# Hybrid decoder layer on one core: constant matmuls ahead of the first block, x scaled by column halves, and the last block's final weight units taken one token half after the other

## What is computed

```python
xn   = rms_norm(x, attn_norm)
proj = xn @ w_in                       # 2048 -> 7184 columns, for two groups of heads
h = x + concat(gated_deltanet(...), moba_attention(...)) @ w_o
hn = rms_norm(h, ffn_norm)
h = h + (silu(hn @ w_gate) * (hn @ w_up)) @ w_down
gate = sigmoid(rms_norm(h, ple_norm) @ w_ple_gate)
out = h + gate * (p @ w_ple_proj)      # p: 256 tokens x 256
```

## Time and profile before

| | |
|---|---|
| median of 3 runs | 1355.14 us (1354.77 to 1355.86) |
| time of the profiled execution | 1352.64 us |
| its span in the profile | 1350.9 us |
| PE busy | 1329.8 us, 98% of the span, 7295 matmuls |
| DVE busy | 797.7 us, 59% |
| ACT busy | 608.8 us, 45% |
| HBM | 237.45 MB read, 2.10 MB written, 177 GB/s over the span |

### The profile page before, as it was taken

One profiled execution on the slowest core, in us unless ns is written; L12 is line 12 of the kernel. 1 busy time (PEld: TensorE's weight loads), 2 busy tenths in 40 slices (PEclk: granted clock), 3 DMA queues, 4 the chain that ended last, 5 costly groups with the idle time before them and its releaser, 6 DMA issues.

```text
span 1350.9 us, 19215 instructions
## 1 busy us (share of the span) xinstructions
PE 1329.8 (98%) x7295; PEld 1124.1 (83%) x7295; DVE 797.7 (59%) x996; ACT 608.8 (45%) x756; POOL 60.7 (4%) x71
## 2 busy tenths in 40 slices
PE   7999999999999999999999999999999999999998
PEld 5999987887888888888888888888888888888886
DVE  6657887589667555555555554454555555555554
ACT  6456533452445545444444443434444444454442
POOL 4102000031110000000000000000000000000000
PEclk9999999999999999999999999999999999999999
DMA  7645454544444756666666656666666666555563
GB/s 240 185 148 172 144 179 134 141 140 139 128 125 141 236 184 187 192 191 180 195 192 187 185 192 193 191 198 191 195 188 189 190 187 187 181 193 188 186 198 129
DMA packets 126366, 240.52 MB, mean 178 GB/s; under 512 B 9743, under 2 KB 10050, under 8 KB 126298
## 3 DMA queue, kind: packets, MB, share of 16 engines
q1 hardware_dynamic: 125108, 237.46, 58.1%
q10 hardware_dynamic: 1190, 2.12, 0.5%
HBM read 237.45 MB, written 2.10 MB: 177 GB/s over the span
## 4 chain that ended last, share of the span: by engine, by line
PE 92%; DVE 5%; ACT 1%; issue 1%; DVEq 0%; ACTq 0%
PE pair L511 26%; PE pair L513 25%; PE pair L512 25%; PE pair L714 3%; PE pair L715 3%; PE pair L716 3%; PE bg L615 2%; DVE w_lo L1117 1%; PE bg L680 1%; PE bg L767 1%; PE bg L556 1%; ACT w_hi L835 0%; DVE mn L1351 0%; PE bg L595 0%; DVE mn L1272 0%
## 5 line engine op out<-in xcount | busy, mean ns | idle before, releaser
L1117 DVE TENSOR_TENSOR w_lo<-raw,w_hi 128x1024 fp32r<-128x1024 f32 x444 | 541.6, 1225 | 420.8 <-ACT w_hi L835 417.9
L835 ACT ACTIVATE w_hi<-raw 128x1024 fp32r<-128x1024 f32 x444 | 468.0, 1060 | 495.7 <-PE pair L513 457.5
L511 PE MATMUL pair<-w_hi,xT_hi 128*128 128x512 f32 x1088 | 431.7, 397 | 0.0
L513 PE MATMUL pair<-w_hi,xT_lo 128*128 128x512 f32 x1088 | 424.1, 390 | 0.0
L512 PE MATMUL pair<-w_lo,xT_hi 128*128 128x512 f32 x1088 | 423.7, 389 | 0.0
L513 PEld LDWEIGHTS pair<-w_hi,xT_lo 128*128 128x128 f32 x1088 | 204.2, 188 | 43.3
L511 PEld LDWEIGHTS pair<-w_hi,xT_hi 128*128 128x128 f32 x1088 | 204.4, 188 | 41.5
L512 PEld LDWEIGHTS pair<-w_lo,xT_hi 128*128 128x128 f32 x1088 | 204.5, 188 | 40.1
L511 PE MATMUL pair<-w_hi,actT_hi 128*128 128x512 f32 x352 | 137.7, 391 | 0.0
L513 PE MATMUL pair<-w_hi,actT_lo 128*128 128x512 f32 x352 | 137.1, 389 | 0.0
L512 PE MATMUL pair<-w_lo,actT_hi 128*128 128x512 f32 x352 | 137.0, 389 | 0.0
(11 more groups left out here) (223 smaller groups left out, 953.6 us busy)
## 6 DMA issues: line engine op xcount, KB each, us to landing
raw<-in_w_in_dram SPq DMA_DIRECT2D x112, 512.0 KB, 3.8
raw<-in_w_gate_dram SPq DMA_DIRECT2D x88, 512.0 KB, 4.4
raw<-in_w_up_dram SPq DMA_DIRECT2D x88, 512.0 KB, 3.8
raw<-in_w_down_dram SPq DMA_DIRECT2D x88, 512.0 KB, 4.7
raw<-in_w_o_dram SPq DMA_DIRECT2D x32, 512.0 KB, 4.9
raw<-in_w_ple_gate_dram SPq DMA_DIRECT2D x32, 512.0 KB, 4.6
raw<-in_w_ple_proj_dram SPq DMA_DIRECT2D x4, 512.0 KB, 7.4
h<-in_x_dram SPq DMA_DIRECT2D x4, 512.0 KB, 8.5
```

What stands on the lines that cost most here:

```text
L511: mm(banks[t][:], hi[:, ts], wh, start=first, stop=False)
L513: m = mm(banks[t][:], lo[:, ts], wh, start=False, stop=last)
L835: f(w_hi[j % RING][:], raw[j % RING][:], ACT.Copy).then_inc(hi_ready, 1)
L1117: v.tensor_tensor(w_lo[j % RING][:], raw[j % RING][:], w_hi[j % RING][:].bitcast(F32), ALU.subtract).then_inc(lo_ready, 1)
```

## The change

At the beginning, PE issues 5 constant matmuls (128x128 by 128x128, float32) before the transposes of `p` and 10 behind them. The units 0 to 3 are split by k tiles (two instructions of 512 columns on ACT and on DVE in place of one of 1024), and PE starts the first k tile of a block once its own low part is ready. The squares of x are made by column halves: ACT takes both of token half 1 and the first of token half 0, DVE the second of token half 0. DVE scales token half 0 and ACT token half 1, each in two column halves, and the groups x0 to x3 wait for the first halves alone, x4 to x7 for the second. POOL adds the two half sums itself. `pp` of block 2 is copied by ACT alone. The groups of transposes are spread: x0 and x1 behind the first k tile of unit 3, x2 behind its second, and x3 to x7 behind one k tile each of units 4, 5 and 6.

At the end, the last four units of the last block are taken first for token half 0 and then for token half 1, and the last token half is finished in two pieces of 256 columns, each with its own DMA.

```diff
     for g in range(KT // 2):
-        at[U_QKV - 1 + g // 4][g // 2 % 2].append(("x", g))
+        i = max(g - 1, 0)
+        at[U_QKV - 1 + i // 2][i % 2].append(("x", g))
...
+LAST_PIECES = ((0, 0, CB), (1, 0, CB // 2), (1, CB // 2, CB))
...
-            for t in range(NT):
-                sp.wait_ge(out_ready, NT * 3 + t + 1)
-                sp.dma_start(out_d[:, t, 3 * CB:], h[:, t, 3 * CB:]).then_inc(out_landed, 16)
+            for n, (t, lo, up) in enumerate(LAST_PIECES):
+                sp.wait_ge(out_ready, NT * 3 + n + 1)
+                sp.dma_start(out_d[:, t, 3 * CB + lo:3 * CB + up], h[:, t, 3 * CB + lo:3 * CB + up]).then_inc(out_landed, 16)
...
-                pool.wait_ge(x_sq[t], 1)
-                rstd(x_rs[:, t:t + 1], x_ms[:, t:t + 1], x_ss[:, t:t + 1], 1.0 / D, EPS, x_rstd, t)
+                pool.wait_ge(x_sq[t], 2)
+                g.tensor_scalar(x_ms[:, t:t + 1], x_half[t][:, 0:1], x_half[t][:, 1:2], EPS, ALU.add,
+                                ALU.add).then_inc(x_rstd, 1)
+                pool.wait_ge(x_rstd, 2 * t + 1)
+                g.tensor_tensor(x_rs[:, t:t + 1], x_ms[:, t:t + 1], half[:, 0:1], ALU.pow).then_inc(x_rstd, 1)
...
-                        if b == 0:
-                            pe.wait_ge(x_scaled, NT)
+                        if b % 4 == 0:
+                            pe.wait_ge(x_scaled[b // 4], NT)
...
-            for s in FIRST:
-                burst(s)
+            def warm_up(count):
+
+                for _ in range(count):
+                    mm(pair[1][1][:, 0:P], ones[:], ones[:], start=True, stop=True)
+
+            pe.wait_ge(masks_ready, 3)
+            warm_up(5)
+            burst(("p", 0))
+            warm_up(10)
             for b in range(4):
                 if b >= 2:
                     wait_pair_read(pe, B_PP + b - 2)
-                use(U_PP + b)
+                pe.wait_ge(k0_lo, b + 1)
                 for k in range(KU):
+                    if k:
+                        use(U_PP + b)
...
-            straight(U_PG, B_PG, 4, UPB, normed)
+            straight(U_PG, B_PG, 3, UPB, normed)
+
+            last_pair = pair[(B_PG + 3) % 2]
+            pe.wait_ge(pair_free[(B_PG + 3) % 2], 2 * ((B_PG + 3) // 2))
+            for j in range(UPB - RING):
...
+            for t in range(NT):
+                ts = slice(t * P, t * P + P)
+                for j in range(UPB - RING, UPB):
+                    if t == 0:
+                        use(UNITS - UPB + j)
+                    for kk in range(KU):
+                        k = KU * j + kk
+                        wh, wl = w_hi[j % RING][:, kk, :], w_lo[j % RING][:, kk, :]
+                        mm(last_pair[t][:], xT_hi[:, k, ts], wh, start=False, stop=False)
+                        mm(last_pair[t][:], xT_hi[:, k, ts], wl, start=False, stop=False)
+                        last = mm(last_pair[t][:], xT_lo[:, k, ts], wh, start=False, stop=(k == KT - 1))
+                last.then_inc(pg_full, 1)
...
             post("p", 0)
-            split(0, 0)
-            split(1, 1)
-            for q in range(2):
-                act.wait_ge(x_landed[0][q], 16)
-            f(x_junk[:, :], h[:, 0, :], ACT.Square, accum_out=x_ss[:, 0:1]).then_inc(x_sq[0], 1)
+            split_k(0)
+            split_k(1)
+            x_square(0, 0)
+            pp_end(0)
             post("gains", 0)
-            split(2, 2)
-            pp_end(0)
-            act.wait_ge(x_rstd, 2)
-            f(h[:, 0, :], h[:, 0, :], ACT.Copy, scale=x_rs[:, 0:1]).then_inc(x_scaled, 1)
+            split_k(2)
+            x_square(1, 0)
+            x_square(1, 1)
             pp_end(1)
-            split(3, 3)
-            for g in range(2):
-                post("x", g)
-            pp_end(2)
+            split_k(3)
+            x_scale(0)
             split(4, 0)
-            for g in range(2, 4):
-                post("x", g)
+            pp_end(2, 1)
+            post("x", 0)
+            x_scale(1)
+            post("x", 1)
             split(5, 1)
+            post("x", 2)
             pp_end(3)
...
             post("p", 0)
-            split(0, 0)
-            split(1, 1)
+            for k in range(KU):
+                split_k(0, k)
+            for k in range(KU):
+                split_k(1, k)
+            a, b = slice(0, D // 2), slice(D // 2, D)
+            dve.wait_ge(x_landed[0][1], 16)
+            v.tensor_tensor_reduce(x_junk2[:, b], h[:, 0, b], h[:, 0, b], 1.0 / D, 0.0, ALU.mult, ALU.add,
+                                   x_half[0][:, 1:2]).then_inc(x_sq[0], 1)
             pp_end(0)
-            split(2, 2)
...
+            for k in range(KU):
+                split_k(2, k)
+            dve.wait_ge(x_rstd, 2)
+            v.tensor_scalar(h[:, 0, a], h[:, 0, a], x_rs[:, 0:1], None, ALU.mult).then_inc(x_scaled[0], 1)
+            v.tensor_scalar(h[:, 0, b], h[:, 0, b], x_rs[:, 0:1], None, ALU.mult).then_inc(x_scaled[1], 1)
             pp_end(1)
-            split(3, 3)
-            dve.wait_ge(x_rstd, 4)
-            v.tensor_scalar(h[:, 1, :], h[:, 1, :], x_rs[:, 1:2], None, ALU.mult).then_inc(x_scaled, 1)
+            for k in range(KU):
+                split_k(3, k)
+            split(4, 0)
             for g in range(2):
                 post("x", g)
-            pp_end(2)
-            split(4, 0)
-            for g in range(2, 4):
-                post("x", g)
             split(5, 1)
+            post("x", 2)
             pp_end(3)
```

More of the change, by code:

```diff
@@ L238, in build @@
         root = sb("root", [P, HG])
-        x_ss, x_ms, x_rs = (sb(n, [P, NT]) for n in ("x_ss", "x_ms", "x_rs"))
-        x_half = sb("x_half", [P, 2])
+        x_ms, x_rs = (sb(n, [P, NT]) for n in ("x_ms", "x_rs"))
+        x_half = [sb(f"x_half{t}", [P, 2]) for t in range(NT)]
         q_ss, q_ms, k_ss, k_ms, k_len, k_inv, k_fac, o_ss, o_ms, o_rs = (
@@ L282, in build @@
         ff_full, ff_free = [sem("ff_full0"), sem("ff_full1")], [sem("ff_free0"), sem("ff_free1")]
-        pg_mul, out_ready = sem("pg_mul"), sem("out_ready")
+        pg_mul, out_ready, pg_full = sem("pg_mul"), sem("out_ready"), sem("pg_full")
         def where(step):
@@ L813, in normed @@
                 return xT_hi[:, k, :], xT_lo[:, k, :]
-            straight(U_PG, B_PG, 4, UPB, normed)
+            straight(U_PG, B_PG, 3, UPB, normed)
+            last_pair = pair[(B_PG + 3) % 2]
+            pe.wait_ge(pair_free[(B_PG + 3) % 2], 2 * ((B_PG + 3) // 2))
+            for j in range(UPB - RING):
+                u = UNITS - UPB + j
+                use(u)
+                for kk in range(KU):
+                    k = KU * j + kk
+                    last = k_tile(u, kk, xT_hi[:, k, :], xT_lo[:, k, :], last_pair, k == 0, False)
+                last.then_inc(unit_used, 1)
+            for t in range(NT):
[3 more added lines that the diff above has]
+                        use(UNITS - UPB + j)
+                    for kk in range(KU):
+                        k = KU * j + kk
+                        wh, wl = w_hi[j % RING][:, kk, :], w_lo[j % RING][:, kk, :]
[3 more added lines that the diff above has]
+                last.then_inc(pg_full, 1)
         @block.scalar
@@ L942, in post, with pp_end, split_k, x_square @@
                     f(om_hi[:, b, :], bk[:, 0:TOK], ACT.Copy).then_inc(om_hi_ready, 1)
-            def pp_end(b):
+            def pp_end(b, last=0):
                 wait_block(act, U_PP + b)
-                f(pp[:, 0, b * CB:(b + 1) * CB], pair[b % 2][0][:], ACT.Copy).then_inc(pair_free[b % 2], 1)
-            post("p", 0)
-            split(0, 0)
-            split(1, 1)
-            for q in range(2):
-                act.wait_ge(x_landed[0][q], 16)
-            f(x_junk[:, :], h[:, 0, :], ACT.Square, accum_out=x_ss[:, 0:1]).then_inc(x_sq[0], 1)
+                for t in range(last + 1):
+                    f(pp[:, t, b * CB:(b + 1) * CB], pair[b % 2][t][:], ACT.Copy).then_inc(pair_free[b % 2], 1)
+            def split_k(b):
+                act.wait_ge(raw_landed[b], 16)
+                f(w_hi[b][:, 0, :], raw[b][:, 0, :], ACT.Copy).then_inc(k0_hi, 1)
+                f(w_hi[b][:, 1, :], raw[b][:, 1, :], ACT.Copy).then_inc(hi_ready, 1)
+            def x_square(t, q):
+                act.wait_ge(x_landed[t][q], 16)
+                junk_x = (x_junk, x_junk2)[t - q][:, q * (D // 2):(q + 1) * (D // 2)]
+                f(junk_x, h[:, t, q * (D // 2):(q + 1) * (D // 2)], ACT.Square, scale=float(D) ** -0.5,
+                  accum_out=x_half[t][:, q:q + 1]).then_inc(x_sq[t], 1)
+            def x_scale(q):
+                cs = slice(q * (D // 2), (q + 1) * (D // 2))
+                act.wait_ge(x_rstd, 4)
+                f(h[:, 1, cs], h[:, 1, cs], ACT.Copy, scale=x_rs[:, 1:2]).then_inc(x_scaled[q], 1)
+            post("p", 0)
+            split_k(0)
+            split_k(1)
+            x_square(0, 0)
+            pp_end(0)
             post("gains", 0)
-            split(2, 2)
-            pp_end(0)
-            act.wait_ge(x_rstd, 2)
```

(33 more changed lines are left out.)

18 lines of the change are left out of this document (8 added, 10 removed).

## The result

The changed kernel takes 1347.49 us (median of 4 executions, 1346.84 to 1348.44) against 1355.30 of before; the ratio is 0.9944 with an interval of 0.9931 to 0.9956. The forecast was 1349.6, in a range of 1348.0 to 1352.4: the right sign, but a gain of 7.8 us for a forecast of 5.6. The same kernel, timed again in two other jobs, gave 1349.34 (0.9954, 0.9940 to 0.9968) and 1349.12 (0.9958, 0.9944 to 0.9972). So there are two questions: what the gain is made of, and why the same kernel gives medians 1.9 us apart. The profiled execution of the changed kernel took 1347.94 us; the forecast for it was 1347.0.

The account below looks back on a forecast made before the run. ACT's chain from 13.5 us was taken to bound the beginning. Beginning 4.1 us plus end 1.5 made 5.6, taking the profiled 1352.64 to 1347.0; with 2.5 us up to the median, 1349.6, range 1348.0 to 1352.4.

Parts of the forecast that it names:

- I carry the same difference over: Whole kernel: 2.5 us between the profiled execution and the median of before, added to 1347.0 to give 1349.6.
- half a microsecond on its lower side: Range for 8 in 10: half a microsecond of run spread below the forecast's own 1348.7, giving 1348.0.
- ACT is what bounds: Beginning: ACT's list from 13.5 us sets when unit 4 starts, 21.9 in place of 26.41.
- The splits, where the forecast weighed a rule: Beginning: no split loss on ACT, 0.07 each on DVE; by the skill's fixed-latency rule the beginning would be worth about 3.0.
- The constant matmuls are worth little by themselves: Projection at the start: the constant matmuls hide ahead of the first low part, cost nothing and gain little alone.
- 1 us or more to spare even with a late clock: PE in the projection: slack of 1 us or more before block 3, even if the clock rises late.
- the start is worth: Beginning: unit 4 starts at 21.9 in place of 26.41, 4.5 us earlier, before 0.44 is given back.
- One group of transposes more, 0.44: Between unit 4 and the block's end: five groups x3 to x7 in place of four, giving back 0.44 us.
- Feeding units 5 and later: After unit 4: ACT and DVE deliver units 5 to 8 in time, the tightest with 0.8 us to spare.
- The end: Behind PE's last matmul: shorter DVE steps save 1.3 us, the last DMA 0.2; sum 1.5, between 1.1 and 1.8.
- The slower one: Rival: clock stays at 1.2 GHz through the projection, total 1.5 us above before, up to 4.4; chance 0.04.
- The deferred work: Rival: DVE's list between 22 and 29 us runs longer, units 5 and 6 stall PE; 1352.6, within 0.2%; chance 0.13.

Follow-up runs that it names:

- before, again: Kernel before, no edit, eleven further executions: 1352.55 to 1355.66 us, ratio 0.9994.
- constant matmuls alone: Kernel before with only the 15 constant matmuls added (5 ahead of the transposes of p, 10 behind); median 1353.86 us, ratio 0.9990.
- end alone: Kernel before with only the end of the change (last four units by token halves, last half in two pieces); median 1353.14 us, ratio 0.9986.
- before, sixteen: Kernel before with 16 constant matmuls issued ahead of PE's 2.2 us wait near 305 us; median 1355.56 us, ratio interval 0.9997 to 1.0015.
- before, nine: Kernel before with 9 constant matmuls ahead of PE's wait near 305 us; 1352.85 to 1354.46 us in 11 executions, mean 1353.78.
- changed, again: Changed kernel, no edit, timed in the second job; median 1349.34 us, ratio 0.9954.
- changed, third: Changed kernel, no edit, timed in the third job; median 1349.12 us, ratio 0.9958.
- beginning alone: Changed kernel with its end put back to that of the kernel before; median 1350.05 us, ratio 0.9966.
- changed, sixteen: Changed kernel with 16 constant matmuls ahead of PE's wait near 305 us; median 1348.43 us, ratio interval 0.9939 to 0.9966.
- changed, nine: Changed kernel with 9 constant matmuls ahead of PE's wait near 305 us; median 1347.44 us, ratio 0.9946.
- changed, eight: Changed kernel with 8 constant matmuls ahead of PE's wait near 305 us; median 1347.10 us, ratio 0.9943.
- no k split: Changed kernel with units 0 to 3 split in one instruction again and PE waiting for both k tiles; median 1348.41 us, ratio 0.9955.
- transposes put back: Changed kernel with the transposes of x placed as in the kernel before; median 1348.17 us, ratio 0.9946.
- no constant matmuls: Changed kernel without its 15 constant matmuls at the start; median 1349.45 us, ratio 0.9957.

## Why the prediction was wrong

All profiled executions side by side give the answer. Landings are the time of issue plus the time to landing, good to 0.1 us. "Low level until" is the start of the first matmul at the high level; it is empty where the constant matmuls had raised the clock before block 0. The constant matmuls in the wait cost 1.8 to 1.9 us (sixteen), 0.3 (nine) and 0.1 (eight) of the last column:

| run | unit 3 landed | unit 4 started | difference | low level until | unit 4 to PE's last matmul |
|---|---|---|---|---|---|
| before | 16.1 | 26.41 | 10.3 | 11.3 | 1317.86 |
| before, again | 17.1 | 27.37 | 10.3 | 12.3 | 1317.81 |
| constant matmuls alone | 17.2 | 27.56 | 10.4 | | 1319.41, fall |
| end alone | 16.0 | 27.60 | 11.6 | 13.3 | 1319.40, fall |
| before, sixteen | 16.0 | 27.68 | 11.7 | 13.5 | 1319.72 |
| before, nine | 16.1 | 26.84 | 10.7 | 11.8 | 1318.13 |
| changed | 17.0 | 23.03 | 6.0 | | 1318.27 |
| changed, again | 17.1 | 23.25 | 6.1 | | 1319.84, fall |
| changed, third | 15.2 | 21.33 | 6.1 | | 1318.23 |
| beginning alone | 15.7 | 21.79 | 6.1 | | 1319.77, fall |
| changed, sixteen | 15.3 | 21.36 | 6.1 | | 1320.11 |
| changed, nine | 17.5 | 23.64 | 6.1 | | 1318.58 |
| changed, eight | 15.6 | 21.74 | 6.1 | | 1318.39 |
| no k split | 15.3 | 22.08 | 6.8 | | 1318.24 |
| transposes put back | 16.7 | 23.03 | 6.3 | | 1319.56, fall |
| no constant matmuls | 15.6 | 22.81 | 7.2 | 12.0 | 1319.74, fall |

*The step that failed* is "I carry the same difference over": 2.5 us between the profiled execution of before and its median, taken as a constant of the measurement. It is three draws. Unit 3 lands between 15.2 and 17.5. The clock rises between 11.3 and 13.5, which costs the kernel before up to 1.3 us and the changed one nothing. And behind the wait near 305 us the clock falls in some executions, for 1.5 to 1.6 us. The profile that I built on had drawn well on the last two. For the profiled execution itself the forecast holds: 1347.0, and 0.9 more as unit 3 landed at 17.0 and not at 16.1, is 1347.9, against 1347.94; that the start came 0.2 later than forecast and the end brought 0.2 more, so that the two cancel, is luck. The median of the first four executions lay 0.45 below that execution and not 2.5 above it. These four had drawn well too: three are at a mean granted clock of 1.000, which no profiled execution with the fall shows (0.997 to 0.999), and the fourth, 1348.44, is at 0.999, which occurs with and without it. The range allowed half a microsecond on its lower side; three executions of before between 1354.77 and 1355.86, with a profile outside them, were a sign that the spread was wider. With all 14 executions the changed kernel's median is 1348.78, inside the range, and the 82 of before have 1355.05: 6.3 us.

*ACT is what bounds: right.* The forecast had unit 4 5.8 us behind unit 3's landing, 21.9 for a landing at 16.1; it is 6.0 to 6.1 in all seven profiles that keep the whole beginning, at landings from 15.2 to 17.5. In all seven unit 4 starts 5.87 to 5.89 us behind ACT's first copy of unit 3 (17.16 in the lines above). The rest is that ACT comes to this copy 0.2 to 0.3 us after the landing, since the copy of `pp` 1 still stands ahead of it. The splits, where the forecast weighed a rule, cost little: ACT's two halves start 0.52 apart, 1.04 together against 0.97; the 0.48 of the forecast had been read from copies of `pp`, another operation. The Trainium skill's rule (VectorE: DVE Perf Modes, the errata section) has the right sign, at 0.07 a split and not its full latency.

*"The constant matmuls are worth little by themselves": wrong.* The forecast gave PE 1 us or more to spare even with a late clock. Its own numbers don't bear that out: with block 0 at the low level to 12.3 and 2.8 us for each of the next two, block 2 ends at 17.9, and block 3 was to start at 17.5. Without them the profile shows PE idle for only 0.24 us ahead of block 3. And the forecast did not ask what in ACT's queue waits for block 0. In the changed kernel the copy of `pp` 0 stands there ahead of unit 2, and ACT waits for block 0 to end; with the low level until 12 this costs 1.1 us. In the kernel before it is `gains` that waits for block 0: of the five executions without constant matmuls at the start, by 0.44, 1.23 and 1.27 us in those whose clock rose at 11.8, 13.3 and 13.5, and not at all in the other two (11.3; and 12.3, where x had landed late). In all five unit 4 starts 13.13 or 13.14 us behind the copy of unit 2, which follows `gains`. So the start is worth 10.3 - 6.1 = 4.2 us in the draw of the profile that the forecast used, for a forecast of 4.5, and 4.8 in the mean of the five (10.9 - 6.1).

The Trainium skill says that the moment of the rise varies from run to run with the same kernel (TensorE: Matmul & The Clock Gate, Part 1), and here it does, by 2 us. The same section of the Trainium skill calls the ramp's price under 1% of a kernel, and the runs agree; here it is at most 0.1% (1.3 us), which is a fifth of the gain. I also took the length of a constant matmul as half of what it is, 0.11 to 0.13 for 0.24: it is two records, and a row that counts 8 of them holds 4. So they are not always hidden: in the profile with eight in the wait they hold PE until 8.3, 1 us after the first low part is made (7.3). It cost unit 4 nothing there.

*One group of transposes more, 0.44: right in size.* 1318.27 - 1317.86 = 0.41.

*Feeding units 5 and later: right.* PE is busy without a wait from 23.03 to 100 us.

*The end: mechanism right, size 1.73 for 1.5.* The DVE steps are as counted (1.28 for 1.3). The last DMA brought 0.45 where I took 0.2: 1.9 us to landing for 128 KB against 2.3 for 256 KB.

*The sum, mended:* 4.8 - 0.4 + 1.7 = 6.1, against 6.3 by the medians of all executions (6.4 by the means). The falls are about even in both kernels and are no part of it: filling the wait brings about 1.2 us in the mean in both, once what the fill costs is added (before: 0.92 with nine and 0.3; changed: 1.14 with eight and 0.1). These means are over executions of several jobs, so they are good to a few tenths.

*The rivals.* The slower one needed the clock low through the whole projection. A low stretch inside the projection does occur, in the run with the constant matmuls alone, but it ended at 20.5. Its price was also too small: a half unit takes 1.5 us at the high level, so a unit at the low one costs about 3 us more and not 1.4. The deferred work didn't catch up.

*What stays open.* Why unit 1 lands at 7.1 to 9.6 us, and all behind it 1 to 2 us apart, wasn't tested. Nor is it shown what decides whether the clock falls behind the wait near 305 us; it is in 6 of the 11 profiled executions with the bare wait, and in none of the 5 with a fill. That the pause is needed for it is shown by these profiles and by the times of the kernels with eight and nine, whose 21 executions (11 of the kernel before, 10 of the changed one) hold none of the upper cluster.

## What to carry to other kernels

Before a forecast of a few microseconds is built on one profile, compare that execution's time with the spread of the others, and ask which draws it contains: landings, the moment at which the clock rises, a pause behind which it may fall. When work on one engine is called hidden, look at what stands behind it in the queues of the engines that read its result, and not only at its own slack. A short wait of PE in a full stretch can cost nearly twice its length (here 2.2 us and 1.6 on top); constant matmuls that fit inside it took the 1.6 away here, and must be counted by their real length.

## What was not expected of the hardware

Behind one wait of 2.2 us, in a kernel that keeps PE busy for 98% of its time, the clock falls to 0.50 in some executions and stays at 1.00 in others, with the same work around it; 1.5 to 1.6 us each time. The wait itself is the same in all of them (2.18 to 2.21 us). In the run with the constant matmuls alone the clock fell behind a wait of 2.1 us at 14 to 17 us, though PE had been at the high level since 8.4. And the granted clock shows 1.00 in stretches at the start in which the matmuls are 0.43 us apart (7.90 to 11.40 in the earlier trace rows): ahead of the first rise the distance of the starts has to be read, not the clock's column.
